# Query projections and scores of heads 2 to 7 moved behind the first twelve expert pairs, one projection a pair

## The reference

```python
q = (xb @ w_q).reshape(TOK_BLOCK, PEER_HEADS, 2, PEER_DHALF)     # 8 heads, 2 halves of 128
s = jnp.einsum('thcd,hcnd->thcn', q, sub_keys)                   # 128 scores for each half
top_s, top_i = lax.top_k(s, K)                                   # K = 16
cand = top_s[:, :, 0, :, None] + top_s[:, :, 1, None, :]
best_s, best_c = lax.top_k(cand.reshape(TOK_BLOCK, PEER_HEADS, K * K), K)
...
e = (i1 * PEER_NKEYS + i2).reshape(TOK_BLOCK, PEER_HEADS * K)    # 128 experts for each token
gate = jax.nn.softmax(best_s, axis=-1)
act = jax.nn.gelu(jnp.einsum('td,ted->te', xb, expert_u[e]), approximate=False)
y = jnp.einsum('te,ted->td', gate * act, expert_v[e])
```

## Time and profile before

| | |
|---|---|
| timed runs | median 2852.82 us of 3 (2851.8 to 2857.2) |
| profiled execution | 2856.23 us, of which the span of the trace is 2854.4 us |
| mean granted clock of TensorE | 0.973 |
| TensorE matmuls busy | 2290.9 us (80%) |
| VectorE busy | 1666.8 us (58%) |
| ScalarE busy | 856.8 us (30%) |
| GpSimd busy | 844.2 us (30%) |
| DMA | 908.03 MB, mean 318 GB/s |
| gathers of expert rows | 768, 805.36 MB, 68.2% of 16 DMA engines' span |

### The profile page before, as it was taken

How to read it: one execution, slowest core, us unless ns; L and a number is a source line. 1 busy time by engine, 2 the same in 40 slices (tenths; PEclk the granted TensorE clock), 3 DMA queues, 4 the chain that set the end, 5 groups by cost and what they waited for, 6 DMA issues and landing times.

```text
span 2854.4 us, 25509 instructions
## 1 busy us (share of the span) xinstructions
PE 2290.9 (80%) x7846; PEld 1258.5 (44%) x7846; DVE 1666.8 (58%) x3913; ACT 856.8 (30%) x2550; POOL 844.2 (30%) x804
## 2 busy tenths in 40 slices
PE   7989898777787778999777777778799777777776
PEld 6889765222242225766222243224657322222322
DVE  2852243677767663253776767764523677777764
ACT  2222013332333332322323333332422233333332
POOL 0022012444434441011444434441001444344442
PEclk9999799999999999989999999999999999999999
DMA  5410157999999996337999999997236999999997
GB/s 181 133 52 16 37 199 300 421 421 421 421 365 422 421 421 257 126 125 298 421 422 421 421 376 417 421 421 294 73 122 230 418 421 421 421 416 421 413 420 295
DMA packets 140454, 908.03 MB, mean 318 GB/s; under 512 B 15616, under 2 KB 16656, under 8 KB 41888
## 3 DMA queue, kind: packets, MB, share of 16 engines
q0 software_dynamic: 110592, 805.36, 68.2%
q1 hardware_dynamic: 29728, 101.06, 10.6%
HBM read 905.30 MB, written 1.05 MB: 318 GB/s over the span
## 4 chain that ended last, share of the span: by engine, by line
DMA 42%; PE 42%; DVE 7%; ACT 5%; issue 4%; POOL 1%; DVEq 0%; POOLq 0%; ACTq 0%
DMA arena<-in_uv,idx 42%; PE bank L1503 15%; PE bank L327 11%; PE bank L698 4%; DVE arena L1451 4%; ACT arena L1478 1%; PE bank L545 1%; PE bank L681 1%; PE bank L1288 1%; PE bank L1303 1%; PE bank L1705 1%; PE bank L531 1%; ACT arena L1466 1%; ACT arena L1472 1%; PE bank L1574 0%
## 5 line engine op out<-in xcount | busy, mean ns | idle before, releaser
L1503 PE MATMUL bank<-arena 128*128 128x512 f32 x3072 | 1441.4, 614 | 475.4 <-ACT arena L1478 469.0
L1520 POOL DMA_INDIRECT arena<-in_uv,idx x768 | 809.2, 1054 | 1771.7 <-PE bank L1503 1201.3
L1503 PEld LDWEIGHTS bank<-arena 128*128 128x128 f32 x3072 | 564.4, 193 | 1348.5 <-ACT arena L1478 754.8
L1451 DVE CUSTOM_DVE_ANT_0 arena<-arena,h 128x1024 f32<-128x1024 f32 x512 | 627.3, 1225 | 372.4 <-DMA arena<-in_uv,idx 370.3
L1466 ACT ACTIVATE arena<-arena 128x2 f32<-128x2 f32 x384 | 78.0, 203 | 1234.0 <-DVE arena L1451 1233.9
L1451 DVE CUSTOM_DVE_ANT_0 arena<-arena 128x1024 f32<-128x1024 f32 x256 | 313.6, 1225 | 188.6 <-DMA arena<-in_uv,idx 186.0
L327 PE MATMUL bank<-xT,weights 128*128 128x256 f32 (+1 forms) x1616 | 364.2, 387 | 0.9 <-ACT xT L746 0.9
L327 PEld LDWEIGHTS bank<-xT,weights 128*128 128x128 f32 x1616 | 309.3, 193 | 49.7 <-issue 2.1
L1478 ACT ACTIVATE arena<-const,arena 128x128 f32<-128x128 f32 x768 | 261.0, 386 | 13.5 <-PE bank L1503 13.4
L1472 ACT ACTIVATE arena<-arena 128x1 f32<-128x1 f32 x768 | 184.8, 288 | 12.6
L1111 POOL TENSOR_TENSOR arena<-arena 128x512 f32<-128x512 f32 (+1 forms) x32 | 34.7, 1108 | 209.0 <-DVE arena L979 185.4
(11 more groups left out here) (319 smaller groups left out, 1721.2 us busy)
## 6 DMA issues: line engine op xcount, KB each, us to landing
weights<-in_w_q SPq DMA_DIRECT2D x48, 512.0 KB, 7.6
weights<-in_w_in SPq DMA_DIRECT2D x38, 512.0 KB, 3.5
arena<-in_uv,idx POOLq DMA_INDIRECT x768
weights<-in_a_fm SPq DMA_DIRECT2D x14, 512.0 KB, 3.2
rows<-in_rows SPq DMA_DIRECT2D x10, 512.0 KB, 4.9
weights<-in_w_o SPq DMA_DIRECT2D x8, 512.0 KB, 3.3
weights<-in_a_out SPq DMA_DIRECT2D x8, 512.0 KB, 3.3
weights<-in_b_fm SPq DMA_DIRECT2D x8, 512.0 KB
```

The costliest lines, as they stand in the source:

```text
L1451: V.tensor_tensor_reduce(out=u, in0=u, in1=x[:, unit // PH, :], scale=1.0, scalar=0.0, op0=ALU.mult, op1=ALU.add, accum_out=dots[:, unit % ...
L1503: ins = nc.tensor.matmul(acc[:, :], diag[:, e % DIAGS, :], ring[:, e % RING, at:at + 512], start=first, stop=last)
L1520: nc.gpsimd.indirect_dma_start(out=ring[:, s, :], out_offset=None, in_=io[f"uv{n}"], in_offset=bass.IndirectOffsetOnAxis(ap=idx[:, unit % ...
```

## The change

The functions that issue projections and scores for TensorE and ScalarE become coroutines: each yields the number of an expert pair (its slot) before a projection and before the scores. A class `Beside` runs such a coroutine up to a given slot. `peer_tensor` calls it behind each pair's matmuls, `peer_scalar` behind each pair's diagonals. Groups 0 and 1 have slot -1 and run before the stream as before. Groups 2, 3 and 4 have the slots 0 to 3, 4 to 7 and 8 to 11 on TensorE: one projection each, and the scores of the group behind its fourth. On ScalarE the copies of group 2 have the slots 0 to 3 too, with those of its scores in slot 3; those of groups 3 and 4 stand one slot later, 5 to 8 and 9 to 12.

```diff
+EARLY_GROUPS = 2
...
+class Beside:
+    def __init__(self, places):
+        self.places, self.at = places, -1
+
+    def run(self, slot):
+        while self.at is not None and self.at <= slot:
+            self.at = next(self.places, None)
...
+        def q_slot(group, step):
+            if group < EARLY_GROUPS:
+                return -1
+            return 4 * (group - EARLY_GROUPS) + step
...
         def peer_scores_tensor(pe, n):
...
-            for lo, hi in Q_GROUPS[1:]:
+            for group in range(1, len(Q_GROUPS)):
+                lo, hi = Q_GROUPS[group]
                 for j in range(lo, hi):
+                    yield q_slot(group, j - lo)
                     fm_tile(pe, ("q", n, j), ("w_q", n, j), xT[:, :, 0:TOK], TOK)
+                yield q_slot(group, 3)
                 pe.wait_ge(*landed(("keys", n, lo)))
...
         def peer_scores_scalar(act, n, name):
...
                 for j in range(lo, hi):
+                    yield q_slot(group, j - lo) + (group > EARLY_GROUPS)
                     act.wait_ge(*banks.full(("q", n, j)))
...
+                yield q_slot(group, 3) + (group >= EARLY_GROUPS) * (group > EARLY_GROUPS)
                 for i in range(NT):
                     score_out(lo, hi, i)
-                if lo == 2:
+                if group == 1:
                     softmax_exp(act, n * UNITS)
...
-        def peer_scalar(act, n):
+        def peer_scalar(act, n, name):
+            beside = Beside(peer_scores_scalar(act, n, name))
+            beside.run(-1)
...
+                    beside.run((unit * PK + kx) // GROUP)
                     if kx == 2 * GROUP and unit < UNITS - 1:
                         softmax_exp(act, n * UNITS + unit + 1)
...
         def peer_tensor(pe, n):
+            beside = Beside(peer_scores_tensor(pe, n))
+            beside.run(-1)
...
                     ins.then_inc(sem("v_used"), 1)
+                    if kx % GROUP == GROUP - 1:
+                        beside.run((unit * PK + kx) // GROUP)
```

More of the change, by code:

```diff
@@ L2096, in _ @@
             for n, mixer in enumerate((two_tensor, three_tensor, None)):
-                peer_scores_tensor(pe, n)
                 peer_tensor(pe, n)
@@ L2114, in _ @@
             for n, mixer in enumerate((two_scalar, three_scalar, None)):
-                peer_scores_scalar(act, n, ("w_o", "a_out", "b_out")[n])
-                peer_scalar(act, n)
+                peer_scalar(act, n, ("w_o", "a_out", "b_out")[n])
                 experts_scalar(act, n, 1)
```

## The result

The changed kernel takes 2881.74 us (median of 4 runs, 2879.53 to 2890.26), before 2855.01 us (4 runs, 2851.8 to 2857.78). The ratio is 1.0100, 95% interval 1.0075 to 1.0124: slower, by 26.7 us at the medians; the forecast was 2879 us and +25.9.

A forecast was written before the change was run, and what follows sets the result against it. Expert-row transfers and TensorE were taken to bound the kernel about equally, in turn. Start 427.7 + pairs 84.0 + scores 8.1 + hand-offs 12.9 + clock 4.5 put pair 12 at 537.2: +8.6 us a layer, +25.9 in all, 2879 us (2860 to 2902).

The forecast's parts named there:

- What bounds: Expert-row transfers rule from 483.5 us, TensorE's projections before; 22 us of transfer time per layer unused from 411 to 472.
- The start: First expert matmul of layer 0 on TensorE at 427.7 us, 39.9 us earlier than before.
- The twelve pairs: First twelve pairs on TensorE, each with a projection: 12 x 7.00 = 84.0 us, plus 8.1 us of scores.
- The hand-offs: TensorE's waits before pairs 1 to 4, through ScalarE's copies and VectorE's scores: 12.9 us a layer in sum.
- The clock: Half clock on TensorE after idle, 1.5 us each at the start and before pairs 3 and 4: 4.5 us a layer.
- the slower rival: Half clock at all four hand-offs and 3.9 us at the start: 2895, up to 2905 us; chance 0.12.
- The sum: Layer 0: pair 12 at 537.2 us, dot product 32 at 546.8 against 538.17 before; +8.6 us a layer.
- the restart: Transfers restarting after pair 12: 2.0 us until a slot is freed, then 7.6 us from gather issue to dot product.
- level: Break-even: pair 12 at 528.6 us, hand-offs and clock together 8.8 us instead of 17.4.
- The rival of no change: Cheap restart (5.5 us), no clock loss before pairs 3 and 4, shorter wait before pair 3: 2853 us; chance 0.07.
- The faster rival: Hand-offs hidden, only TensorE's pairs and projections count: pair 12 at 521.3, -7.3 us a layer, 2831 us; chance 0.13.

The follow-up runs named there:

- the seventh kernel: Changed kernel with group 2 before the stream, groups 3 and 4 at one projection every second pair, all their ScalarE copies one pair later: 2789.60 us.
- the third kernel: Changed kernel with group 2 before the stream and all ScalarE copies and scores of groups 3 and 4 one pair later: 2814.48 us.
- the first kernel: Changed kernel with ScalarE's first three copies of group 2 one pair later, the fourth copy and the scores unmoved: 2849.09 us.
- the fourth: Changed kernel with groups 3 and 4 spread to one projection every second pair, group 2 as in the changed kernel: 2855.54 us.
- the sixth kernel: Changed kernel with 24 added matmuls a layer on TensorE before pair 0, their result overwritten: 2875.68 us.

## Why the prediction was right

**What bounds.** Right: from 411 to 472 us the transfers had 22 us to give, and the seventh kernel gained 21.7 a layer.

**The start.** 427.7 forecast; 430.04 less 2.3 is 427.7.

**The twelve pairs.** A pair and a projection 7.00 forecast; 6.88 without a gap (485.94 less 482.49 is 3.45 for the projection, and 3.43 for a pair that follows directly; the 3.54 of the forecast was read from a pair that stands behind an idle gap of 1.37 us).

**The hand-offs.** 1.7, 1.7, 4.9 and 4.6 us forecast (the last is 4.5 by its own rows, 452.4 less 447.88). From the end of a projection's 3.46 us, or of the scores, to the next pair: 1.5, 1.5, 4.9 and 4.5. None at pairs 5 to 11. The first and the third kernel show that the gaps before pairs 1 to 3 are a cost and not only beside it.

**The clock.** 4.5 us forecast, 5.8 measured in layer 0 (1.7, 1.7, 2.4), and more in layers 1 and 2, where the row of pair 0 is 5.7 and 6.2 us long against 5.45 in layer 0. The price of one gap was sized too small: the five pairs of 19.13 us in the earlier trace rows lie 1.7 us, and not 1.5, above what they take at full clock when the four that follow directly are counted at 3.43. The gaps of 1.4 us didn't lower the clock (granted 1.00 from 441 to 445 and from 449 to 453 us), as the stretch of before at 1.00 had it. They are not such waits as the Trainium skill tells of in "TensorE: Matmul & The Clock Gate", section "HAM oscillation — how this bites in real kernels": its loop waits some 3 to 5 us in each round. So the slower rival, which charged all four hand-offs, was wrong for two of them, and its 9.9 us were not reached.

**The sum.** Pair 12 at 537.2 forecast and 537.2 measured. That these agree is luck, since errors cancel: the pitch is 0.8 too much (seven of the twelve pairs follow directly and take 0.11 less), the hand-offs 0.5 too much, the clock 1.3 too little. Dot product 32 at 546.8 forecast, 547.77 less 2.3 = 545.5 measured: the restart from pair 12 takes 8.2 us and not 9.6. Its gather is issued at 542.19 us, 2.7 us behind pair 12 and not 2.0, and its dot product follows 5.6 us later and not 7.6. Per layer +8.6 forecast, +6.4, +9.3 and +8.4 measured; the rest of the program gives 0.6.

**What it didn't see.** It had one loss, hand-offs and clock of 17.4 us where 8.8 would have been level. The runs find two losses that add: three of the hand-offs, with the half clock behind the third, are worth 32.7 us (the first kernel), the dense projections of pairs 5 to 11 26.2 us (the fourth), and taking away either alone gives a kernel about level with before. The single sum came out all the same; a position on TensorE hides where the transfers lose their time. It mattered as soon as I used the position for another kernel (the fourth), and I was off by 30 us.

The rival of no change had a restart of 5.5 us from gather to dot product, and 5.6 was measured, but it also needed the clock to hold and a shorter gap before pair 3, and neither came. The faster rival fell with the measured gaps; its own mechanism is real, and the third and seventh kernels are what it looks like when nothing stands between a projection and the next pair. What stays open: how much of the 4.4 us gap before pair 4 is on the path by itself; no run took it away alone.

## What to carry to other kernels

When work of one engine is moved into a stream that another resource limits, look first at the engine that stands between them. Here the copy on ScalarE sat one place too early in an in-order queue, and put TensorE's projection into the loop from transfer to diagonal; one place later no gap is left behind it. Then give the moved work out at a pace at which the limiting transfers stay full: one projection every second pair is worth 25 us more here than one a pair. And judge by bytes moved in a stretch, not by when an engine starts: 40 us of earlier start moved no more bytes here in the first 79 us.

## What was not expected of the hardware

Gaps of the same length on TensorE lower its clock in one place and not in another: behind 2.35 us of idle pair 0 took 5.40 us in layer 0 and 3.70 in layers 1 and 2 of the sixth kernel. And an activation table is paid where it is reloaded: putting the exp ahead of the copy hid its own load, and the 1.28 us of the gelu's came behind the copy, with a gap of 2.79 us.
